# Two slots instead of three for streamed weight blocks, and one more row buffer for gathers

## What is computed

```python
def peer_ffn(h, wq, k1, k2, u, v):          # channel mixer, once a layer
    q = (t @ wq).reshape(n_tok, 8, 2, 128)  # 8 heads, two halves
    s1, s2 = q[:, :, 0] @ k1.T, q[:, :, 1] @ k2.T
    ...                                      # top 16 of each, top 16 of the 256 sums: idx, gate
    act = gate * gelu(einsum('nd,nkd->nk', t, u[idx]))
    y = einsum('nk,nkd->nd', act, v[idx])    # 128 experts (8 heads x 16) for each token

for i in range(2):
    x = x + gt1 * mixer_i(rmsnorm(x) modulated)
    x = x + gt2 * peer_ffn(rmsnorm(x) modulated)
return rmsnorm(x, final_norm_g)
```

## Time and profile before

| | us |
|---|---|
| median of 3 runs | 1930.86 (1923.73 to 1937.14) |
| the profiled execution's own time | 1922.51 |
| its span, first to last instruction | 1920.7 |
| TensorE busy | 1527.7 (80%) |
| VectorE busy | 1334.4 (69%) |
| GpSimd busy | 584.6 (30%) |
| ScalarE busy | 419.1 (22%) |
| moved by DMA | 703.32 MB, mean 366 GB/s |
| mean granted TensorE clock | 0.88 of 2.4 GHz |

### The profile page before, as it was taken

How to read it: one execution, slowest core, us unless ns; L and a number is a source line. 1 busy time by engine, 2 the same in 40 slices (tenths; PEclk the granted TensorE clock), 3 DMA queues, 4 the chain that set the end, 5 groups by cost and what they waited for, 6 DMA issues and landing times.

```text
span 1920.7 us, 22276 instructions
## 1 busy us (share of the span) xinstructions
PE 1527.7 (80%) x7828; PEld 920.6 (48%) x7828; DVE 1334.4 (69%) x3962; ACT 419.1 (22%) x1139; POOL 584.6 (30%) x551
## 2 busy tenths in 40 slices
PE   7999899776757979888889687998889875655555
PEld 7644675433213757656557265765656631111111
DVE  5767656868886779675445777877844579778655
ACT  1212201000002722622211264154120210000001
POOL 0011133344442322322322322232232244454441
PEclk9999799677677999999899899999999897776877
DMA  9888589999998977987999997699699999999995
GB/s 370 338 321 321 195 353 421 421 421 419 419 421 336 421 287 259 420 329 278 401 409 410 407 407 316 234 388 369 236 393 397 413 366 421 421 422 420 422 422 221
DMA packets 100255, 703.32 MB, mean 366 GB/s; under 512 B 15264, under 2 KB 15648, under 8 KB 16560
## 3 DMA queue, kind: packets, MB, share of 16 engines
q0 software_dynamic: 78336, 570.46, 73.6%
q1 hardware_dynamic: 21808, 131.45, 16.9%
HBM read 700.82 MB, written 1.05 MB: 365 GB/s over the span
## 4 chain that ended last, share of the span: by engine, by line
PE 39%; DMA 25%; DVE 16%; issue 5%; ACT 4%; POOL 1%; DVEq 0%; POOLq 0%; ACTq 0%
PE PS L1648 15%; DMA ub<-in_peer_uv,idx 10%; DMA vb<-in_peer_uv,idx 9%; PE PS L1798 3%; PE PS L2015 3%; PE PS L1991 3%; DMA ring<-in_peer_uv,idx 3%; PE PS L1704 2%; PE PS L1972 2%; DVE vb L1149 2%; DVE ub L1149 2%; DMA mods<-in_peer_uv,idx 2%; PE PS L1875 1%; DMA ring<-in_gdn_z 1%; PE PS L1893 1%
## 5 line engine op out<-in xcount | busy, mean ns | idle before, releaser
L1648 PE MATMUL PS<-ub,z 128*64 128x512 f32 x832 | 321.4, 752 | 110.6 <-DVE z L1115 110.4
L1648 PE MATMUL PS<-vb,z 128*64 128x512 f32 x816 | 309.2, 739 | 122.1 <-DVE z L1115 114.8
L2052 POOL DMA_INDIRECT ub<-in_peer_uv,idx x208 | 232.3, 1117 | 493.1 <-PE PS L1648 424.4
L2052 POOL DMA_INDIRECT vb<-in_peer_uv,idx x204 | 218.2, 1070 | 469.4 <-PE PS L1648 419.3
L1361 ACT ACTIVATE tanhs<-cubed 128x2 f32<-128x2 f32 x256 | 52.0, 203 | 872.2 <-DVE cubed L1104 871.2
L1648 PEld LDWEIGHTS PS<-vb,z 128*64 128x64 f32 x816 | 71.5, 158 | 267.7 <-DVE z L1115 173.2
L1648 PEld LDWEIGHTS PS<-ub,z 128*64 128x64 f32 x832 | 74.4, 161 | 260.8 <-DVE z L1115 166.2
L1149 DVE CUSTOM_DVE_ANT_0 ub<-ub,h 128x1024 f32<-128x1024 f32 x104 | 127.1, 1222 | 46.6 <-DMA ub<-in_peer_uv,idx 45.7
L1149 DVE CUSTOM_DVE_ANT_0 vb<-vb,h 128x1024 f32<-128x1024 f32 x102 | 124.8, 1223 | 39.6 <-DMA vb<-in_peer_uv,idx 38.9
L1108 DVE SCALAR_TENSOR_TENSOR acts<-tanhs,gated_x 128x2 f32<-128x2 f32 x256 | 40.6, 159 | 152.6 <-ACT tanhs L1361 152.5
L1648 PE MATMUL PS<-mods,z 128*64 128x512 f32 x208 | 125.9, 736 | 23.3 <-DVE z L1115 23.0
(11 more groups left out here) (364 smaller groups left out, 2800.9 us busy)
## 6 DMA issues: line engine op xcount, KB each, us to landing
ring<-in_gdn_qkv SPq DMA_DIRECT2D x32, 1024.0 KB, 9.7
ring<-in_peer_wq SPq DMA_DIRECT2D x23, 1024.0 KB, 9.9
two_slots<-in_ada_wide POOLq DMA_DIRECT2D x20, 1024.0 KB, 6.3
ring<-in_gdn_z SPq DMA_DIRECT2D x16, 1024.0 KB, 9.8
ring<-in_gdn_w_out SPq DMA_DIRECT2D x16, 1024.0 KB, 9.4
ring<-in_gla_w_in SPq DMA_DIRECT2D x6, 2048.0 KB, 9.4
mods<-in_ada_wide POOLq DMA_DIRECT2D x11, 1024.0 KB, 6.6
ring<-in_ada_w SPq DMA_DIRECT2D x4, 2048.0 KB, 11.8
```

What stands on the lines that cost most here:

```text
L1648: last = pe.matmul(y[64 * g:64 * g + 64, e, :], z[:, i % 4, g, :], rows[:, D + e * 512:D + (e + 1) * 512], start=False, stop=False, skip_g ...
L2052: pool.indirect_dma_start(row_buffers[b], None, uv_rows, off).then_inc(row_landed[b].sem, 16)
```

## The change

The blocks from number 4 on alternate between slots 0 and 1. The load of block n waits for the use of block n - 2; for blocks 4 and 5 that is the use of blocks 0 and 1. Block 2 is the only one that still lies in slot 2. Its 8 KB a partition become row buffer 9, so the two in `area` are now 10 and 11: 12 buffers in stretches 0 and 3, 10 in stretches 1 and 2. The new buffer is the last in the first round (`FIRST`), and gather 11, its first user, waits on GpSimd until three blocks have been used.

```diff
-        row_landed = [signal(f"rows_landed{i}") for i in range(11)]
+        row_landed = [signal(f"rows_landed{i}") for i in range(12)]
         def g_slot(n):
-            return n if n < 4 else n % 3
+            return n if n < 4 else n % 2
         def g_turn(n):
-            return 1 if n < 4 else n // 3 + (n % 3 > 0)
+            return 1 if n < 4 else n // 2
...
             if n >= 4:
-                sp.wait_ge(g_used.sem, n - 2)
+                sp.wait_ge(g_used.sem, n - 3 if n < 6 else n - 1)
...
-            row_buffers += [mods[:, 0:2, :].rearrange("p a d -> p (a d)")] + [area[:, 2 * i * D:(2 * i + 2) * D] for i in (1, 2)]
+            row_buffers += [mods[:, 0:2, :].rearrange("p a d -> p (a d)"), ring_flat[:, 2 * 2048:3 * 2048]] + [area[:, 2 * i * D:(2 * i + 2) * D] for i in (1, 2)]
...
-            FIRST = (0, 1, 2, 3, 8, 9, 10, 4, 5, 6, 7)
+            FIRST = (0, 1, 2, 3, 8, 10, 11, 4, 5, 6, 7, 9)
...
-                    free = range(11 if n // STRETCH in (0, 3) else 9)
+                    free = range(12 if n // STRETCH in (0, 3) else 10)
...
+                            if n == 11:
+                                pool.wait_ge(g_used.sem, 3)
```

## The result

The change makes the kernel slower by 3%: 1984.79 us (median of 4, 1983.09 to 1988.31) against 1927.3 us (median of 4, 1919.47 to 1937.14) on the same chip, a ratio of 1.0307 with a 95% interval of 1.0269 to 1.0344. That is +57 us where +22 was forecast. The mean granted clock of TensorE is 0.880 and 0.878.

What follows compares the result with a forecast made beforehand. Stretches 0 and 3 bound by bytes at 421 GB/s, z, out and wq1 by TensorE and DMA together; 32 + 6 - 5 - 6 - 2.5 - 2.5 = +22 us, added to the median: 1953 us, range 1920 to 1985.

Steps and rivals of the forecast that it cites:

- The landing time: L, a weight block's time from issue to landing in the z, out and wq1 stages, taken as 7.5 us.
- The two rivals at 5.5 and 9.7 us: Landing at most 5.5 us: weights cost nothing, 1912 us, chance 0.12; landing staying at 9.7: 1992 us, chance 0.13.
- the 6.5 of the third: Rival: slower stages shrink the gather backlog, landings settle near 6.5 us; +2, 1933 us, chance 0.35.
- Two slots suffice: Rival: landing at most 5.5 us, weights cost nothing and the buffer's gains are left; -16, 1912 us, chance 0.12.
- The idle time: TensorE's waits for weights: z loses 6 us, out 6 and wq1 4, 16 us a tile.
- The stage term: Cost of two slots in the z, out and wq1 stages of both tiles: 32 us in all.
- L + 3.7: A slot's round trip with two slots: landing time L plus the block's own use, against 9.2 us of TensorE's work.
- The in stages: Second in block shares its slot with ab and lands 2.2 and 3.8 us late: +6 us, from 0 to 10.
- The added buffer: Tenth row buffer in stretches 1 and 2: rows ready sooner in the second in stages, -5 us, between 0 and -6.7.
- The end of stretch 1: Rows late there would be ready if the mixer comes later, absorbing delay: -6 us, between 0 and -8.
- Stretch 3: One more gather done at its start, then bytes alone at 421 GB/s: -2.5 us, from 0 to -2.5.
- Stretch 0: Second in block no longer loaded in it, 1 MB less before its end: -2.5 us.

Runs made afterwards that it cites:

- the slots alone: Two weight slots as in the change, but no added row buffer (11 and 9 as before), against the kernel before: 1982.44 us, ratio 1.0297.
- fillers: The change with 10 small products without use ahead of blocks that TensorE waits for: 1982.15 us; with 4 of them: 1985.68 us.

## Why the prediction was wrong in size

The direction and the mechanism held: TensorE, in order, waits for a slot's round trip. Point by point:

- **The landing time** held, roughly. 7.5 us assumed; the nine landings on the chain through tile 0's stages took 7.8 in the mean, the seven through those of tile 1 8.5. With the slots alone the medians of all loads in the three stages are 7.8, 6.7 and 7.0. The two rivals at 5.5 and 9.7 us are both out; the 6.5 of the third is near the medians of two stages, but not the landings that are waited for. "Two slots suffice" would also have been what the Trainium skill's advice to double-buffer gives (Trainium Kernel Development and Optimization, Best Practices); here the step from three slots to two costs 3%.
- **The idle time** held, in part by luck. In tile 0 TensorE idles 6.1, 6.6 and 5.1 us more than before in the z, out and wq1 stages, 17.8 together; 16 was forecast. But the forecast's z term counts from a stage without idle time, while the z stage before already idled 1.6 us, so its own rule gives 4.4 there. That the slow products lengthen the round trip was not in it.
- **The stage term was mis-sized: 32 forecast, 56 measured.** This is the step that failed. The sum counted the idle time and no change in the products: in L + 3.7 it held a block's own use at 3.7 us. Behind a long enough wait a block takes 5.4 us (at 918.30 and 1011.52), at a granted clock of 0.50. In the trace of after this follows each of the seven waits for weights of 3 us and more, four of the six from 1.97 to 2.74 us, and none of 1.72 us or less. Over the three stages of tile 0 the products take 7.8 us longer. 17.8 + 7.8 = 25.6, against 26.5 for the three stages of tile 0 by the table. In tile 1 the same windows give about 20 us more idle time and 9 us more of products, against 29.2. So of the 24 us that the term lacked some 17 are slow products and 6 idle time. The prediction had the lower clock as an addition to its worst rival, up to 10 us a tile, and left it out of the forecast, though 2 us waits at every second block, which it did forecast, can bring it. The chain shows that the slow products set the end of the z stage; what the kernel would gain by keeping the clock up could not be separated by fillers.
- **The in stages: +6 forecast, -5 from the tenth buffer; +12 and +2 measured.** The block behind ab is waited for 2.47 and 3.26 us in the two tiles, near the forecast's 2.2 and 3.8, but its products then take 5.33 and 6.69 us instead of 3.84: the same step that failed. With the block loaded early about half of the 12 is still left. That fits the round trips of the later blocks, which the steps between them were said to hide. In the second in stage the buffer's gain did not come, and with two slots the chain runs there through weights.
- **The added buffer: -5 forecast, nothing measured**, with and without it 1984.8 and 1982.4 us. The idea that a buffer is worth something was sound one step lower, where it is worth 20 us. That the tenth adds nothing in total beside two slots is shown, to within the intervals of about 7 us; why is not. It does shorten VectorE's waits for rows, from 163 us over all buffers with the slots alone to 142 with it. For the largest kind of dot product they fall from 43.9 to 32.8 us. The row of each:

```profile
L1149 DVE CUSTOM_DVE_ANT_0 ub<-ub,h 128x1024 f32<-128x1024 f32 x104 | 127.2, 1223 | 43.9 <-DMA ub<-in_peer_uv,idx 43.0
```

```profile
L1149 DVE CUSTOM_DVE_ANT_0 ub<-ub,h 128x1024 f32<-128x1024 f32 x94 | 115.0, 1224 | 32.8 <-DMA ub<-in_peer_uv,idx 32.0
```

  There are 94 instead of 104 in the second, since the new buffer takes a share, but that is a tenth of the count for a quarter of the wait. That these waits were not on the way to the end is argued, not shown.

- **The end of stretch 1: -6 forecast, +0.2 measured.** The forecast took the late rows there for a backlog that a delay lets drain. The chain shows a buffer's round trip: pair, issue, 9.87 us of landing. That does not shrink when everything before it comes later.
- **Stretch 3** held: -2.9 us for -2.5, and the plateau of 421 GB/s stays. It is the same in the other launches: the piece behind wq1 of tile 1 takes 370.0 to 374.0 us in the six profiled launches with 12 buffers there, 373.6 to 375.9 in the four with 11, 379.6 to 380.6 in the three with 10. **Stretch 0** can't be told: -2.8 us for -2.5 is less than launches that do the same there differ by. That gather 11 waits for a third block shows no cost.

By these sizes the sum is 22 + 24 (stages) + 13 (in stages and buffer) + 6 (end of stretch 1) - 2 (the other pieces) = +63 for the profiled pair, which differs by 62.1; the 1 is rounding.

## What to carry to other kernels

Price a slot of a stream by its round trip under the load that the stage really has (landing beside the queued gathers, plus the block's own use) against the consumer's work in one turn of the slots; neither the block's size nor the DMA rate alone gives it, and halving the size bought an estimated 1.3 us of 7.5. When TensorE begins to stall, add to the idle time what its next products lose in speed, and add that to the round trip of what they hold. A resource given is not worth what the same resource taken costs: look for a wait on the critical chain that the gift ends, and if that wait is itself a round trip, don't expect a delay elsewhere to absorb it.

## What the runs showed of the hardware

A landing of 1 MB beside a queue of gathers took 6.7 to 7.8 us with one or two blocks in flight (medians of the z, out and wq1 stages of tile 0, the slots alone) and 9.2 to 10.5 us with up to three (the same stages of the kernel before); the shortest of each run was 4.7 us. 512 KB took 8.6 us with up to four halves in flight. So here what is in flight went with the landing time more than what one transfer carries.

In the trace of after, behind each of the seven waits for weights of 3 us and more, TensorE's next block was slow: products of 128x256 that take 3.72 us took 5.41 us, at a granted clock of 0.50 inside them and of 0.93 to 0.96 over the stages of tile 0. After waits of 1.97 to 2.74 us that was so four times of six, after shorter ones never; with 4 small products ahead of the wait it was so behind 1.68 us too (8.86 us for two blocks). Small products in the waits, 2.5 us each, held it at 0.98 to 1.00.
